# Even mixer on Trainium2: the sample chunk and the finishing norms as one program instead of two

## What is computed

```python
o_a, s_delta = _gated_delta(q, k, v, g, beta, s_delta)    # 4 heads, keys 128, values 128
o_a = (_rms(o_a) * gain_a) * silu(z)
y, s_rwkv = _rwkv7(r, decay, k, v, -kk, kk * a, s_rwkv)   # 8 heads of 64
yc = y - mean(y)                                          # over the 64 of a head
y = yc * rsqrt(mean(yc ** 2) + GN_EPS) * lnx_gain + lnx_bias
y = (y + sum(r * k * r_k) * v) * gb                       # gb = sigmoid(g_lr) @ w_g2
out = concat([o_a, y]) @ w_out_even
```

## Time and profile before

| | us |
|---|---|
| median of 3 runs | 3037.87 (3034.39 to 3042.06) |
| the profiled execution | 3035.05 |
| its span, first to last instruction | 3033.3 |
| PE busy over the span | 2786.5 (92%) |
| DVE / ACT / POOL busy | 1246.8 / 872.4 / 162.1 |
| sample chunk, first instruction to last | 1045.8 to 1160.8 |
| finishing norms | 1165.5 to 1227.2 |
| next dense program, first matmul | 1235.1 |

### The profile page before, as it was taken

One profiled execution on the slowest core, in us unless ns is written; L12 is line 12 of the kernel. 1 busy time (PEld: TensorE's weight loads), 2 busy tenths in 40 slices (PEclk: granted clock), 3 DMA queues, 4 the chain that ended last, 5 costly groups with the idle time before them and its releaser, 6 DMA issues. The chain is left out here.

```text
span 3033.3 us, 52033 instructions
## 1 busy us (share of the span) xinstructions
PE 2786.5 (92%) x23297; PEld 2586.3 (85%) x23297; DVE 1246.8 (41%) x1934; ACT 872.4 (29%) x1254; POOL 162.1 (5%) x195
## 2 busy tenths in 40 slices
PE   3999999998799886799999999999999598899998
PEld 1999988897488863789998999998889478899998
DVE  3333225742666534553332453322543355633324
ACT  3222214224333201342221432221422332422222
POOL 1000001000100000100000000000100111000001
PEclk7999999998699856899999999999999678999999
DMA  5222455622000101332235432235572104322224
GB/s 234 86 83 84 131 190 173 221 80 82 1 3 2 49 29 49 111 126 84 84 100 196 144 126 84 84 114 191 159 254 63 52 5 130 123 83 83 82 82 127
DMA packets 82343, 317.33 MB, mean 105 GB/s; under 512 B 9400, under 2 KB 14408, under 8 KB 80584
## 3 DMA queue, kind: packets, MB, share of 16 engines
q1 hardware_dynamic: 82120, 313.99, 31.1%
HBM read 303.22 MB, written 10.74 MB: 104 GB/s over the span
## 5 line engine op out<-in xcount | busy, mean ns | idle before, releaser
L616 PE MATMUL banks<-h_r,weights_r 128*128 128x288 f32 (+1 forms) x2496 | 563.2, 297 | 30.2 <-DVE big_r L341 22.8
L165 DVE TENSOR_TENSOR weights_r<-work,weights_r 128x1024 fp32r<-128x1024 f32 (+1 forms) x280 | 337.3, 1205 | 552.9 <-ACT weights_r L161 552.6
L620 PE MATMUL banks<-h_r,weights_r 128*128 128x288 f32 (+1 forms) x2496 | 559.7, 296 | 0.0
L161 ACT ACTIVATE weights_r<-work 128x1024 fp32r<-128x1024 f32 (+1 forms) x280 | 290.6, 1038 | 619.6 <-PE banks L620 612.1
L616 PEld LDWEIGHTS banks<-h_r,weights_r 128*128 128x128 f32 x2496 | 410.2, 189 | 48.0 <-issue 32.2
L618 PE MATMUL banks<-low_r,weights_r 128*128 128x288 f32 (+2 forms) x1744 | 424.2, 298 | 0.0
L618 PE MATMUL banks<-big_r,weights_r 128*128 128x288 f32 x1888 | 419.4, 295 | 0.0
L620 PEld LDWEIGHTS banks<-h_r,weights_r 128*128 128x128 f32 x2496 | 409.6, 189 | 0.0
L618 PEld LDWEIGHTS banks<-big_r,weights_r 128*128 128x128 f32 x1888 | 308.4, 189 | 0.1
L618 PEld LDWEIGHTS banks<-low_r,weights_r 128*128 128x128 f32 x1744 | 298.7, 190 | 0.4
L616 PE MATMUL banks<-h_r,ring_r 128*128 128x288 f32 (+1 forms) x1216 | 277.3, 299 | 3.1 <-DVE ring_r L165 3.1
(11 more groups left out here) (479 smaller groups left out, 3593.5 us busy)
## 6 DMA issues: line engine op xcount, KB each, us to landing
work<-w_ff_dram SPq DMA_DIRECT2D x130, 512.0 KB, 3.6
h<-w_mod_dram SPq DMA_DIRECT2D x48, 768.0 KB, 5.3
work<-w_down_dram SPq DMA_DIRECT2D x66, 512.0 KB, 3.6
consts<-w_ff_dram SPq DMA_DIRECT2D x64, 512.0 KB, 3.6
work<-w_mod_dram SPq DMA_DIRECT2D x32, 768.0 KB, 9.1
work<-w_in_even_dram SPq DMA_DIRECT2D x24, 512.0 KB, 3.7
big_buf<-w_mod_dram SPq DMA_DIRECT2D x16, 768.0 KB, 5.7
consts<-w_down_dram SPq DMA_DIRECT2D x22, 512.0 KB, 3.6
```

Of the source, the lines that this page charges most:

```text
L161: return act.activation(high, raw, ACT.Copy)
L165: return engine.tensor_tensor(low, raw, high.bitcast(F32), ALU.subtract)
L616: pe.matmul(out[a], low[:, w], x[a][0], start=begins, stop=False)
L620: last = pe.matmul(out[a], high[:, w], x[a][0], start=False, stop=closes)
```

## The change

`even_chunks` and `finish_even` become one program, `even_tail`. What it does:

- **Stacking.** Two heads lie above each other, one in partitions 0 to 63, one in 64 to 127. The three streams become one strip of six pairs, so there is one inverse of 12 small products a step (`corners`) where there were three of four. PSUM reads of 64 rows and 3 times 256 columns become reads of 128 rows and 384 columns. `prepare_even` lays the sample columns of `k.cols` in the same way.
- **Prompt norms in the waits.** Mean, squares, sums, roots, spreading and gate of the 512 prompt columns are written in between the steps of the sample chunk, tile by tile (`mean0` to `gate3`); those of the 64 sample columns follow behind (`mean_s` to `gate_s`).
- **Roots by token blocks.** `TokenRoots` packs the sums of 4 tiles, 4 blocks of 128 tokens and 2 halves in 32 partitions of 128 columns, where `InverseRoots` had 4 or 8 partitions of 576.
- **States.** The spread updates have buffers of their own for all heads. DVE makes `Uw`; POOL makes `RVw` and `RUw` and does both decays (`Sg`, `RSd`).
- The transfer that restores `x` and that of `w_g2` are issued inside this program, and one block boundary is gone.

```diff
+    def sums(self, pe, x, bank, tile):
+        pe.wait_ge(self.ready, 1)
+        for c in range(NCH):
+            for t in range(4):
+                i = 4 * c + t
+                last = pe.matmul(bank[0:self.units, 0:P], self.window(x, i, self.units), tile(t)[:, c * P:(c + 1) * P],
+                                 start=i == 0, stop=i == 4 * NCH - 1)
+        return last
...
+    def invert(self, dve, x):
+        return dve.reciprocal(self.inverses[x], self.roots[x])
...
+    def broadcast(self, pe, x, bank, t):
+        for c in range(NCH):
+            i = 4 * c + t
+            last = pe.matmul(bank[:, c * P:(c + 1) * P], self.spread[:, i * P:(i + 1) * P], self.inverses[x],
+                             start=True, stop=True)
+        return last
...
+def even_tail_orders():
+    each = lambda *names: [f"{n}{t}" for t in range(4) for n in names]
+    pe = ["R", "kkq", "vkt", "mean0", "mean1", "mtka", "m", "rbkr", "mta", "mean2", "mean3", "rvb", "rkt", "sq", "sqt",
+          "suma", "bonus0", "x1", "sq2", "bonus1", "bonus2", "ko", "rko", "x2", "bonus3", "spa0", "spa1", "kst", "rw",
+          "spa2", "spa3", "u", "ru", "var", "bonus_s", "o_0", "o_1", "ry", "spy0", "gate0", "spy1", "gate1",
+          "mean_s", "suma_s", "spy2", "gate2", "s0a", "s0b", "s1a", "s1b", "spy3", "gate3", "spa_s", "var_s",
+          "s2a", "s2b", "s3a", "s3b", "spy_s", "gate_s", "rs0", "rs1", "rs2", "rs3"]
...
+                sp.wait_ge(*after("pool", "RSd3"))
+                sp.dma_start(k.io["rwkv_s_out"], RS).then_inc(states_out, 16)
...
+                roots.constants(pool)
+                pool.wait_ge(*after("act", "RVB"))
+                by_sequence("RVw", RVs, Vt)
+                pool.wait_ge(*after("act", "eR"))
+                pool.wait_ge(*after("pe", "ko"))
+                for h in range(4):
...
+                pool.wait_ge(*after("act", "RU"))
+                pool.wait_ge(*after("pe", "var"))
+                by_sequence("RUw", RUs, RU)
...
+                def corners(job, left, right):
+                    b = claim(job)
+                    for t in range(6):
+                        for g in range(2):
+                            at = slice(t * 64, (t + 1) * 64)
+                            last = mm(b[half(g), at], left[half(g), at], right[half(g), at])
+                    done(job, last)
...
+                for t in range(4):
+                    for q in range(NSEQ):
+                        at = slice(q * TS, (q + 1) * TS)
+                        for g in range(2):
+                            last = mm(b[half(g), t, :, at], S4[half(g), t, q], ar4[half(g), t, :, at])
+                done("rko", last)
...
+                pe.wait_ge(*after("pool", "RUw"))
+                for t in range(4):
+                    b = claim(f"rs{t}")
+                    at = slice(t * 64, (t + 1) * 64)
+                    for g in range(2):
+                        mm(b[half(g)], Bt[half(g), at], RUs(t)[half(g)], stop=False)
+                    for g in range(2):
+                        last = mm(b[half(g)], Kt[half(g), at], RVs(t)[half(g)], start=False)
+                    done(f"rs{t}", last)
...
     even_prompt(k)
-    even_chunks(k, sample=True)
-    finish_even(k)
+    even_tail(k)
```

More of the change, by code:

```diff
@@ L1830, in even_jobs @@
[L1830 to L1847, removed]
@@ L1947, in even_chunks @@
+        bank = lambda job: k.psum[number[job] % 8]
         with nc.Block() as block:
@@ new lines, in _ @@
+                done("kkq", last)
+                b = claim("vkt")
+                for t, g, h in heads:
+                    mm(b[half(g), t * P:(t + 1) * P], vc[:, h], ident)
+                    last = mm(b[half(g), 256 + t * P:256 + (t + 1) * P], kc[:, h], ident)
+                done("vkt", last)
+                mean(0)
+                mean(1)
+                pe.wait_ge(*after("dve", "Kq"))
+                b = claim("mtka")
+                scores(b, 0, b_of(0), a_of(0))
+                done("mtka", scores(b, 256, b_of(1), a_of(0)))
@@ new lines, in _ @@
+                b = claim("m")
+                done("m", scores(b, 0, a_of(0), b_of(0)))
+                b = claim("rbkr")
+                scores(b, 0, b_of(0), a_of(1))
+                done("rbkr", scores(b, 256, b_of(1), a_of(1)))
+                pe.wait_ge(*after("dve", "M1"))
+                b = claim("mta")
+                for t, g, h in heads:
+                    at = slice(t * m, (t + 1) * m)
+                    last = mm(b[half(g), at], B0[half(g), at], ident[half(g), half(g)])
@@ new lines, in _ @@
+                b = claim("rw")
+                for t in range(4):
+                    at = slice(t * 64, (t + 1) * 64)
+                    for g in range(2):
+                        mm(b[half(g), at], rko4[half(g), t, 0], ident[half(g), half(g)], stop=False)
+                    for g in range(2):
+                        last = mm(b[half(g), at], KA[half(g), at], Vt[half(g), at], start=False)
+                done("rw", last)
+                spread_a(2)
+                spread_a(3)
+                pe.wait_ge(*after("dve", "W2"))
@@ new lines, in _ @@
+                done("ru", last)
+                pe.wait_ge(*after("act", "sqy3"))
+                b = claim("var")
+                done("var", roots.sums(pe, "y", b, sq_y))
+                b = claim("bonus_s")
+                for t in range(4):
+                    last = mm(b[:, t * m:(t + 1) * m], k.mask("block64"), bonus_s[:, t])
+                done("bonus_s", last)
+                pe.wait_ge(*after("act", "U"))
+                b = [claim(f"o_{g}") for g in range(2)]
+                last = [None, None]
```

1233 lines of the change are left out of this document (505 added, 728 removed), and 3 rows, old and new, of the table dve.

## The result

The change makes the kernel faster. The medians of 4 executions each are 2949.62 us after (2947.01 to 2954.16) and 3036.20 us before; the ratio is 0.9724 (95% interval 0.9712 to 0.9735), 84 us by the ratio. The forecast was 2955, with 2940 to 2986 as its range. The profiled execution took 2954.16 us, the longest of its four.

What follows compares the result with a forecast made beforehand. PE was taken as busiest, mostly at half clock, with waits for DVE. PE's stream 87 us (78 work, 9 clock), waits 5 and tail 6.8 gave 99 against 181.4 us: 2952.5, said as 2955, range 2940 to 2986.

Steps and rivals of the forecast that it cites:

- PE's work, 78 us: PE's products in the new program at the high clock: 36.9 full-height, 23.1 paired, 10.7 ko, 7.5 rko.
- the fourth rival: Better still: half clock only 8 us, fewer waits, delta states overlapping; stretch 89 us, total 2945 or less; below 2940: 0.06.
- What I had at nothing: Changes of matmul shape on PE, taken from the earlier trace to cost nothing that its rows can tell.
- The clock, 9 us: Half clock for the first 10 us and for 9 us behind rko, adding 9 us to PE's stream.
- Waits, 5 us: PE's remaining waits in the new program: 1 for y's reciprocal, about 1.2 for mean3, 3 for handovers.
- The wait of 1 us for `invy`: PE's wait for the reciprocal of y, now 128 columns, not hidden because DVE has other work ahead: 1 us.
- the 3 us for handovers: Allowance for handovers between engines of some tenths of a microsecond each, 3 us in all.
- The tail, 6.8 us: Behind the last matmul: DVE's add 0.69, POOL's decay 1.37 and the state transfer 4.7 us.
- POOL: POOL's RVw, Sg and RUw take 18.6 us in all, ending at 65, before PE reaches rs0 at about 78.
- Half clock nearly throughout: First rival: PE stays at half clock over most of the stretch, 135 us, total about 2991; chance 0.19.
- The drain at a change of shape: Second rival: some 40 changes between full-width and half-width jobs cost 0.25 us each, 10 us, total 2965; chance 0.08.
- POOL was never near the path: Third rival: POOL's broadcasting products far slower, 3047 at 8.5 times; POOL or another wait eating everything: 0.03.

Runs made afterwards that it cites:

- run 2: Changed kernel with only rko's 64 small matmuls issued half by half: 2941.13 us in one execution, 2951.03 us in a series; the unchanged kernel again gave 2949.78 us.
- run 6: Changed kernel with wide prompt products laid between the narrow ko and rko matmuls: 2939.54 us, and 2938.62 us in a second series.
- run 9: Changed kernel with an added DVE reciprocal of 384 columns ahead of invy, its result read by nothing: 2956.10 us in one execution.
- run 4: Changed kernel with state spreads and decays back on DVE, as late as before, instead of early on POOL: 2954.18 us, stretch 110.8 us.
- run 1: Changed kernel with its small products issued one half of the rows after the other instead of in turn: 2956.25 us, stretch 104.6 us.
- run 3: Changed kernel with all prompt norms behind the sample chunk instead of between its steps: 2950.11 us, stretch 98.9 us.
- run 5: Changed kernel with the delta and RWKV states moved ahead of the last prompt norms and the sample norms: 2940.80 us, stretch 96.5 us.
- run 8: Changed kernel with POOL's first job (the constants) held until DVE is past its first sample operations: 2947.83 us, stretch 97.4 us.

## Why the prediction was right

**The total.** 99 us were predicted, 97.6 measured. The agreement is partly luck: the clock's term is 3 us too small and that of the waits 4 us too large, and inside PE's work the parts are off by 5 us in both directions. The last step of the sum was luck as well: I added 2.8 us from the profiled execution to the median, and the median came out 4.5 below the profiled one. The profiled time itself, 2954.2, stood against 2952.5.

- **PE's work, 78 us.** PE was busy for 90.0 us; with the clock's loss taken off (next point) that is 77.7. Inside it the states were priced too high. Two delta states in different halves overlap as the fourth rival had it: 4096 columns took 1.93 + 2.00 = 3.9 us, not 7.4. The RWKV states took 7.1 us, not 8.6 (0.86 ns a column against 1.05). `rko` took 6.9, not 7.5, and `ko` 11.2, not 10.7. This is 5.1 us less, and the small products at 0.93 instead of 1.05 ns would add 1.6 over the prediction's 13568 columns. What I had at nothing fills most of it: the changes of shape, at 0.14 us or more each; at the prediction's count of some 40 that is about 5.6 us. No run tests that count, so this balance is an argument and not a measurement.
- **The clock, 9 us.** It was low for 7.3 us at the start (10 predicted) and for 17.9 us behind `rko` (9 predicted): 3.4 + 8.9 = 12.3 us lost. The place of the fall, early in `ko`, was right; the return was mis-sized, and runs 2 and 6 show that this is the least certain term of the sum.
- **Waits, 5 us.** 1.0 us, that of `mean3` (1.2 predicted). The wait of 1 us for `invy` was hidden (run 9), and the 3 us for handovers did not show.
- **The tail, 6.8 us.** 6.7.
- **POOL.** `RVw`, `RUw` and `Sg` took 16.8 us for 18.6, and `RSd` 1.06 for 1.37. Run 4 shows what this placing is worth.

**The steps behind it.** The turns in the stacked products are worth 7 us (run 1). The prompt norms in the waits are worth 1 us of the stretch (run 3), so the old waits did not go because norms filled them; that they went because the spreading left the loop and the steps became short fits runs 3 and 4, and is not shown apart. Spreading early on POOL is worth up to 13 us (run 4). The boundary and the old tail of the chunk, 6.2 us, went, and the new tail took their place. The single reciprocal of 128 columns took 0.94 us for the old wait of 4.6. By the balance in the section on the result, the 84 us are 42 of waiting, 33 to 34 of clock (mean 0.55 and 0.67 before, 0.77 in the program now) and 8 to 9 of cheaper products. Which part of the change gave the clock, the missing waits or the single inverse with fewer and wider reads, stays open, since these were not undone apart.

**The rivals.** Half clock nearly throughout was wrong: it held for 40 of 91 us, and the last 30 ran at 0.99. The drain at a change of shape was right in kind and too dear: 0.14 to 0.18 us, not 0.25. I had read it as nothing from the earlier trace rows, and that reading was wrong: it sets a pace from start to start (0.24 us) beside L1544 from its start to its end, 1.90 / 8. The next row of that timeline is

```profile
1034.51 0.44 PE L1553 MATMUL banks<-work 128*128 128x128 f32 x2
```

so L1544 took (1034.51 - 1032.78) / 8 = 0.22 us from start to start, and the rows with the change were slower. That a change of tiling mode drains the engine is the rule of the Trainium skill, page "TensorEngine Tiling (Array Packing)", section "Key Properties", and the rows of run 3 agree with it. POOL was never near the path. The better case was right in kind about the delta states (3.5 us less, where it had 2), nearer about the waits, and wrong about the clock, which was low for 25 us outside `ko` and `rko` and not for 8.

## What to carry to other kernels

Before filling waits with other work, ask whether the waits survive the rest of the change: here nearly all of them were gone without the filling, and with the norms behind the chunk the kernel took the same time. Work that prepares a late step belongs on an idle engine as early as its inputs are there, and two halves of the array want their products in turn. When PE is busy without a gap, look at the granted clock next: here it made up most of the fall in PE's busy time (an estimate), and laying wide products between the narrow ones gave another 10 us without removing an instruction, though no run shows that their width is the reason. Take several executions, since how long the clock stays low moves by itself, and so does the time outside the part that was changed.

## What the runs showed of the hardware

- In the changed kernel the granted clock stayed at 0.50 for 33.1 us while PE was busy for 33.1 of them. In the kernel of run 2 it came back at 1093 in one execution and after 1107 in another.
- It fell after 22.0 us of full PE activity at 1.00 (run 5). The Trainium skill, page "TensorE: Matmul & The Clock Gate", section "What's actually happening", ties the clock to how busy PE is; by the busy time of the profile these rows don't follow it.
- DVE stands while POOL works on SBUF: a copy of 0.29 us took 1.65, a product of 0.29 us took 1.87 (run 8).
- A change between 128 and 32 rows costs PE 0.14 to 0.18 us (run 3), and one from 128 to 64 rows 0.14 in the changed kernel.
- Two products of 64 by 64 with 512 columns, in different halves of the array and in turn, took 0.86 ns a column at full clock, and small ones of 64 columns 0.93.
